# Expert layer of a decoder step: fp32 matmuls replaced by three-product split matmuls, with loads of 256 columns

## The chip, the cores and the metric

The kernel runs on one core of a Trainium2 chip. The metric is the device time of one execution in microseconds (us), taken as the median of several runs. Five engines work beside each other and meet only at semaphores: TensorE (PE, matmuls), VectorE (DVE), ScalarE (ACT), GpSimd (POOL) and SyncE (SP, which here only issues DMA transfers). Each engine takes its own instructions strictly in the order in which they are written.

## The reference

The program is one inference step of a two-layer decoder for 512 prompt tokens and 8 sample tokens (520 in all, 1024 channels). The change touches only the channel mixer of the second layer, a top-2-of-8 mixture of SwiGLU experts:

```python
D_MODEL, N_EXPERTS, TOP_K, D_FF_E = 1024, 8, 2, 1408

def swiglu(h, wg, wu, wd):
    return (jax.nn.silu(h @ wg) * (h @ wu)) @ wd

def moe(h, w_router, wg, wu, wd):
    probs = jax.nn.softmax((h @ w_router).astype(F32), -1)
    top_p, top_i = lax.top_k(probs, TOP_K)
    top_p = top_p / jnp.sum(top_p, -1, keepdims=True)
    gates = jnp.sum(jax.nn.one_hot(top_i, N_EXPERTS, dtype=F32) * top_p[..., None], -2).astype(h.dtype)
    out = jnp.zeros_like(h)
    for e in range(N_EXPERTS):
        out = out + gates[..., e:e + 1] * swiglu(h, wg[e], wu[e], wd[e])
    return out
```

All arrays are float32. An expert has two weight matrices of 1024 x 1408 (gate and up) and one of 1408 x 1024 (down), 16.5 MiB in all.

## The kernel before

Tokens are sorted by expert into slots in DRAM. The experts run in **passes**: a pass takes 176 slots (`SLOTS`) of one expert, and with these inputs there are eight. Every engine has its own loop over the passes (`Fori(0, PASSES)` with `If(p < n_passes)`), written out for all of a pass. Nothing is scheduled: the order on each engine is the order of the code.

A pass works with the tokens transposed (channels on the 128 partitions, 176 columns of tokens):

- 22 **gate and up blocks** (11 pairs, block m = 2f is gate f, m = 2f + 1 is up f). A block is a product of 8 channel slices, each a 128 x 128 weight tile times 128 x 176 tokens (`hTe`), added up in one PSUM bank. ACT applies Silu to the gate bank (L2091) and DVE multiplies it with the up bank (L1739) into `acte`.
- The next pass's rows are transposed into banks 6 and 7 (`expert_tokens`, L1132) and copied to `hTe` by ACT (L2094).
- 8 **down blocks**, each a product of 11 slices with `acte` (L1185). DVE copies each result out of its bank (L1743), PE transposes it (`results`, L1175), ACT copies the rows (L2100), and POOL writes the rows of the pass to DRAM.

The matmuls have float32 operands; one such matmul is two MATMUL instructions, each with a weight load (LDWEIGHTS) of its own. Weights come from SP's queue, one block per transfer, into a ring of 11 slots for gate and up (`w_ring`) and of 4 for down (`d_ring`).

The dense mixer of the first layer, earlier in the program, already has a split form, and the change takes its parts over: ACT copies a weight block rounded to fp32r (`high_part`, L1975), DVE subtracts it from the block (`low_part`, L1467), and PE sums three fp32r products of 260 columns (L841, L843, L845): high weights with high and with low tokens, low weights with high tokens. There POOL splits the activations into high and low (L2191, L2194).

Of the kernel before, what the change touches and what calls it, by code (L numbers as in the profile page):

```python
# [17 lines left out]
F32 = mybir.dt.float32  # L18
# [7 lines left out]
P = 128  # L26
# [45 lines left out]
EXPERT_USES = [6, 5, 6, 5, 4, 4, 6, 6]  # L72
EPS = 1e-6
# [22 lines left out]
def build(nc, a, o):  # L96

    (y_prompt, y_sample, p_delta, p_conv, p_ckv, p_kpe, p_mem_k, p_mem_v, s_delta, s_conv, s_ckv, s_kpe) = o
    with ExitStack() as ctx:
# [22 lines left out]
        xT = sb("xT", [P, KT, T])  # L122
        hT = fixed("hT", [P, KT, T])
        w_ring = fixed("w_ring", [P, WS, KT, P])
        memkT = sb("memkT", [P, 2, 2, MEM])
# [158 lines left out]
        acte, q = place(q, FB, SLOTS)  # L284
        sge, q = place(q, 2, SLOTS)
        yTe, q = place(q, KT, SLOTS)
        yrow, q = place(q, 2, D)
        hTe, q = place(q, KT, SLOTS)
        hrow, q = place(q, 2, D)

# [145 lines left out]
        table_in = sem("table_in")  # L436
        page_rows_ready = sem("page_rows_ready")
# [93 lines left out]
        def last_in(ring, m):  # L531

            first, total = (0, 2 * FB) if m < 2 * FB else (2 * FB, KT)
            i = m - first
            return (m - ring, 0) if i >= ring else (first + max(x for x in range(total) if x % ring == i % ring), 1)

# [3 lines left out]
        def _(pe):  # L540
# [346 lines left out]
            loops["parts"] = 0  # L887
            memory_attention(0)
# [252 lines left out]
            while w_turn[0] % WS:  # L1141
                w_turn[0] += 1
            f0, w0, d0 = loops["experts"] = (list(uses), list(w_uses), [2 * loops["parts"] + 1] * DS)
            per = EXPERT_USES
            pe.wait_ge(routed, 4)
            n_passes = pe.value_load(table[0:1, PASSES:PASSES + 1], min_val=1, max_val=PASSES)
            with pe.Fori(0, PASSES) as p:
                with pe.If(p < n_passes):

                    for k in range(2 * FB):  # L1150
                        s, r = k % WS, k // WS
                        f, bk = k // 2, 2 * (k % 2) + k // 2 % 2
# [13 lines left out]
                    for bk in (2, 3):  # L1166
                        pe.wait_ge(bank_free[bk], p * per[bk] + f0[bk] + per[bk])

                    def results(i):
# [4 lines left out]
                        for r in range(2):  # L1174
                            mm = pe.transpose(bank[bk][0:ROWS, r * P:(r + 1) * P], yTe[:, i, r * ROWS:(r + 1) * ROWS], ident)  # L1175
# [3 lines left out]
                    for i in range(KT):  # L1179
                        s, r = i % DS, i // DS  # L1180
                        bk = 4 + i % 2
                        pe.wait_ge(d_loaded[s], p * 32 + 16 * (d0[s] + r))
                        pe.wait_ge(bank_free[bk], p * 4 + f0[bk] + i // 2)
                        for f in range(FB):
                            mm = pe.matmul(bank[bk][:, 0:SLOTS], d_ring[:, s, f * P:(f + 1) * P], acte[:, f, :],  # L1185
                                           start=(f == 0), stop=(f == FB - 1))
                        mm.then_inc(d_used[s], 1)
# [5 lines left out]
        def _(dve):  # L1193
# [535 lines left out]
            f0, w0, d0 = loops["experts"]  # L1729
            per = EXPERT_USES  # L1730
            with dve.Fori(0, PASSES) as p:
                with dve.If(p < n_passes):

                    dve.wait_ge(d_used[DS - 1], p * 2 + d0[DS - 1])
                    for f in range(FB):
                        k, bg, bu = 2 * f + 1, f % 2, 2 + f % 2
                        dve.wait_ge(w_used[k % WS], p * 2 + w0[k % WS] + k // WS + 1)
                        dve.wait_ge(bank_free[bg], p * per[bg] + f0[bg] + f // 2 + 1)
# [778 lines left out]
```

## Time and profile before

| what | value |
| --- | --- |
| median of 3 runs | 2539.14 us (2539.13 to 2541.26) |
| the profiled execution's own time | 2534.16 us |
| its span, first to last instruction | 2532.5 us |
| PE busy over the span | 2220.1 us (88%) |
| DVE, ACT, POOL busy | 766.9, 468.4, 249.1 us |
| the experts' eight passes | 1814.59 to 2484.60 us of the span |
| mean granted clock of TensorE | 0.902 of full speed |

The profile is one execution. A row that groups instructions gives their count and the mean length of one; lengths overlap where an engine is pipelined, so a rate is read from starts that follow each other. A clock of 1.00 is 2.4 GHz and 0.50 is 1.2 GHz.

### The profile page before, as it was taken

The page shows a single profiled execution, that of the slowest core. Times are in us where ns is not written, and L with a number is a line of the kernel's source. Part 1 is how long each engine was busy: PE and PEld are TensorE (multiplying, and loading weights), DVE is VectorE, ACT ScalarE, POOL GpSimd, SP SyncE. Part 2 cuts the span into 40 slices and gives each one's busy share as a digit, 9 for nine tenths or more (in the row PEclk, how much of TensorE's full clock was granted, in tenths as well). Part 3 has the DMA queues.
Part 4 walks back from the last instruction along what each step waited for, and adds up shares of the span by engine and source line. Part 5 has one row for each costly group of instructions (what it writes and reads, how often), then busy time and mean ns, then how long its engine had stood idle before and what let it go on. Part 6 is the DMA issues. An engine that isn't in the chain of part 4 may idle for free.

```text
span 2532.5 us, 33729 instructions
## 1 busy us (share of the span) xinstructions
PE 2220.1 (88%) x13726; PEld 2007.2 (79%) x13726; DVE 766.9 (30%) x1437; ACT 468.4 (18%) x1020; POOL 249.1 (10%) x332
## 2 busy tenths in 40 slices
PE   5899898976769999997898699997699999999992
PEld 4788787864659999996754577776699999999992
DVE  2245555537232222222224366721100000000003
ACT  1133422203022212211123200101201111111101
POOL 0000101020002302300110033200100000000001
PEclk8899999956789999998898689987799999999996
DMA  7222100030213242342060245520788988898883
GB/s 193 67 67 75 36 1 4 1 95 26 83 34 92 72 113 76 88 113 62 29 231 1 67 166 223 193 75 0 197 217 214 272 208 210 210 273 211 210 204 124
DMA packets 452944, 306.00 MB, mean 121 GB/s; under 512 B 22382, under 2 KB 435457, under 8 KB 448705
## 3 DMA queue, kind: packets, MB, share of 16 engines
q1 hardware_dynamic: 433812, 225.74, 34.0%
q0 software_dynamic: 19024, 78.72, 9.1%
q8 instruction: 81, 1.33, 0.2%
q14 instruction: 27, 0.21, 0.0%
HBM read 276.42 MB, written 28.14 MB: 120 GB/s over the span
## 4 chain that ended last, share of the span: by engine, by line
PE 67%; issue 19%; DVE 6%; POOL 4%; DMA 2%; SPq 1%; ACT 1%; POOLq 0%; DVEq 0%; ACTq 0%
PE bank L1156 17%; PE bank L510 13%; PE bank L1185 8%; PE bank L1062 6%; POOL actL L2194 2%; PE bank L690 2%; PE bank L675 1%; PE bank L685 1%; PE bank L1079 1%; PE bank L548 1%; POOL actH L2191 1%; SPq L2303 1%; PE bank L841 1%; PE bank L845 1%; PE bank L843 1%
## 5 line engine op out<-in xcount | busy, mean ns | idle before, releaser
L1156 PE MATMUL bank<-arena,w_ring 128*128 128x176 f32 x2816 | 424.5, 314 | 4.6 <-issue 4.6
L1156 PEld LDWEIGHTS bank<-arena,w_ring 128*128 128x128 f32 x2816 | 422.4, 191 | 6.6 <-issue 6.6
L510 PE MATMUL bank<-hT,w_ring 128*128 128x260 f32 x1600 | 364.0, 390 | 16.3 <-DVE hT L1208 15.1
L510 PEld LDWEIGHTS bank<-hT,w_ring 128*128 128x128 f32 x1600 | 310.1, 194 | 66.4 <-DVE hT L1208 16.0
L1185 PE MATMUL bank<-arena 128*128 128x176 f32 x1408 | 219.6, 313 | 0.0
L1185 PEld LDWEIGHTS bank<-arena 128*128 128x128 f32 x1408 | 210.2, 190 | 0.0
L1777 ACT ACTIVATE arena<-bank 128x512 f32<-128x512 f32 (+4 forms) x200 | 86.7, 454 | 421.8 <-PE bank L510 226.3
L1739 DVE TENSOR_TENSOR arena<-arena,bank 128x176 f32<-128x176 f32 x88 | 29.7, 337 | 431.4 <-PE bank L1156 431.4
L841 PE MATMUL bank<-hH,gu_high 128*128 128x260 f32 x704 | 142.7, 284 | 18.1 <-DVE w_low L1467 18.1
L1062 PE MATMUL bank<-arena 128*128 128x256 f32 x640 | 151.0, 387 | 3.9 <-DVE arena L1597 3.9
L845 PE MATMUL bank<-hH,w_low 128*128 128x260 f32 x704 | 142.5, 284 | 0.0
L843 PE MATMUL bank<-hL,gu_high 128*128 128x260 f32 x704 | 142.3, 284 | 0.0
L1062 PEld LDWEIGHTS bank<-arena 128*128 128x128 f32 x640 | 118.5, 192 | 26.2 <-issue 9.7
L841 PEld LDWEIGHTS bank<-hH,gu_high 128*128 128x128 f32 x704 | 109.2, 189 | 18.6 <-issue 18.6
L845 PEld LDWEIGHTS bank<-hH,w_low 128*128 128x128 f32 x704 | 109.3, 190 | 0.0
L843 PEld LDWEIGHTS bank<-hL,gu_high 128*128 128x128 f32 x704 | 109.1, 189 | 0.0
L2091 ACT ACTIVATE arena<-bank 128x176 f32<-128x176 f32 x88 | 27.9, 317 | 346.3 <-PE bank L1156 346.2
L1467 DVE TENSOR_TENSOR w_low<-w_ring,gu_high 128x1024 fp32r<-128x1024 f32 x44 | 53.5, 1225 | 113.2 <-ACT gu_high L1975 113.2
L1743 DVE COPY arena<-bank 128x176 f32<-128x176 f32 x64 | 21.9, 342 | 212.3 <-PE bank L1185 212.3
L841 PE MATMUL bank<-actH,d_high 128*128 128x260 f32 x352 | 72.3, 288 | 7.5 <-POOL actL L2194 7.5
L843 PE MATMUL bank<-actL,d_high 128*128 128x260 f32 x352 | 72.2, 287 | 0.0
L845 PE MATMUL bank<-actH,d_low 128*128 128x260 f32 x352 | 72.2, 287 | 0.0
(438 smaller groups left out, 2824.7 us busy)
## 6 DMA issues: line engine op xcount, KB each, us to landing
w_ring<-in_we_gate SPq DMA_DIRECT2D x88, 512.0 KB, 7.2
w_ring<-in_we_up SPq DMA_DIRECT2D x88, 512.0 KB, 7.3
arena<-in_we_down SPq DMA_DIRECT2D x64, 704.0 KB, 6.4
w_ring<-in_w_in_a SPq DMA_DIRECT2D x26, 512.0 KB, 3.7
w_ring<-in_w_gate SPq DMA_DIRECT2D x22, 512.0 KB, 3.8
w_ring<-in_w_up SPq DMA_DIRECT2D x22, 512.0 KB, 3.8
arena<-in_w_down SPq DMA_DIRECT2D x16, 704.0 KB, 6.2
slots<-arena POOLq DMA_DIRECT2D x4, 2560.0 KB, 21.8
```

The source lines that it names most:

```text
L510: mm = pe.matmul(out[i][:, 0:hi - lo], w_ring[:, s, kt, :], rhs[:, kt, lo:hi], start=(kt == 0), stop=(kt == KT - 1))
L690: mm = pe.matmul(b[:, c * P:(c + 1) * P], Xs[:, i, c * P:(c + 1) * P], Einv[:, i, c * P:(c + 1) * P], start=True, stop=True)
L841: pe.matmul(out, w_high, x, start=first, stop=False)
L843: pe.matmul(out, w_high, x, start=False, stop=False)
L845: mm = pe.matmul(out, w_low, x, start=False, stop=last)
L1062: mm = pe.matmul(sc[:, half * GC:(half + 1) * GC], Wq[:, n % 2, blk * P:(blk + 1) * P], block_columns(G, blk), start=(blk == 0), stop=(blk ...
L1156: mm = pe.matmul(bank[bk][:, 0:SLOTS], w_ring[:, s, kt, :], hTe[:, kt, :], start=(kt == 0), stop=(kt == KT - 1))
L1185: mm = pe.matmul(bank[bk][:, 0:SLOTS], d_ring[:, s, f * P:(f + 1) * P], acte[:, f, :], start=(f == 0), stop=(f == FB - 1))
L1467: dve.tensor_tensor(low, raw_block, top.bitcast(F32), ALU.subtract).then_inc(split, 1)
L1739: dve.tensor_tensor(acte[:, f, :], sge[:, f % 2, :], bank[bu][:, 0:SLOTS], ALU.mult)\
L1777: act.activation(dst, b[:, 0:dst.free_size()] if src is None else src(b), func, scale=scale).then_inc(free(key), 1)
L2194: pool.tensor_tensor(actL[:, f, lo:hi], sg[:, f % 2, lo:hi], actH[:, f, lo:hi].bitcast(F32), ALU.subtract)\
```

## The change

The expert products go over to the split form. Tokens and activations are kept as a high and a low half side by side (`eh`, `eact`, 2 x 176 columns). For each slice there are two fp32r matmuls: the high weights with both halves (352 columns, one bank) and the low weights with the high half (176 columns). The two halves of a bank are added when it is read, by a `tensor_reduce` on DVE, which replaces the reads by ACT and the copies by DVE. ACT makes the high weights of every block (five buffers, `ex_high`), DVE the low ones in place of the raw block, both four blocks ahead (`EX_AHEAD`). POOL splits the activations. Loads fetch two blocks at a time (256 columns), six slots for gate and up and three for down. On each engine the semaphore `high_free` counts blocks that PE has finished.

```diff
+EX_SLOTS, EX_DOWN, EX_HIGH, EX_OUT = 6, 3, 5, 4
+EX_AHEAD = 4
@@ PE
+            def expert_product(out, low, top, x, first, last, slot_used):
+
+                if first:
+                    pe.matmul(out[:, 0:2 * SLOTS], top, x.rearrange("p a b -> p (a b)"), start=True, stop=False)
+                mm = pe.matmul(out[:, 0:SLOTS], low, x[:, 0, :], start=False, stop=False)
+                if slot_used is not None:
+                    mm.then_inc(slot_used, 1)
+                if not first:
+                    mm = pe.matmul(out[:, 0:2 * SLOTS], top, x.rearrange("p a b -> p (a b)"), start=False, stop=last)
+                if last:
+                    mm.then_inc(high_free, 1)
-                        pe.wait_ge(w_loaded[s], p * 32 + 16 * (w0[s] + r + 1))
+                        pe.wait_ge(split, p * BLOCKS + split0 + m + 1)
                         pe.wait_ge(bank_free[bk], p * per[bk] + f0[bk] + f // 2)
                         for kt in range(KT):
-                            mm = pe.matmul(bank[bk][:, 0:SLOTS], w_ring[:, s, kt, :], hTe[:, kt, :],
-                                           start=(kt == 0), stop=(kt == KT - 1))
-                        mm.then_inc(w_used[s], 1)
+                            expert_product(bank[bk], low[:, kt, :], top[:, kt, :], eh[:, kt], kt == 0, kt == KT - 1,
+                                           w_used[j % EX_SLOTS] if half and kt == KT - 1 else None)
@@ DVE
+            def block_out(p, i, back=0):
+
+                expert_done(dve, p, 2 * FB + i, back)
+                dve.tensor_reduce(yTe[:, i % EX_OUT, :], halves_of(bank[4 + i % 2]), X, ALU.add).then_inc(bank_free[4 + i % 2], 1)
+
+                    def low_part(m):
+                        raw_block, low, top = expert_parts(m)
+                        dve.wait_ge(high, p * BLOCKS + split0 + m + 1)
+                        dve.tensor_tensor(low, raw_block, top.bitcast(F32), ALU.subtract).then_inc(split, 1)
...
+                    for m in range(BLOCKS):
+                        if m + EX_AHEAD < BLOCKS:
+                            low_part(m + EX_AHEAD)
+                        if m < 2 * FB and m % 2 == 0:
+                            f = m // 2
+                            expert_done(dve, p, m)
+                            dve.tensor_reduce(gate_sum[:, f % 2, :], halves_of(bank[f % 2]), X, ALU.add).then_inc(bank_free[f % 2], 1)
+                        if m < 2 * FB and m % 2:
+                            f = m // 2
+                            bu = 2 + f % 2
+                            expert_done(dve, p, m)
+                            dve.tensor_reduce(up_sum, halves_of(bank[bu]), X, ALU.add).then_inc(bank_free[bu], 1)
+                            dve.wait_ge(bank_free[bu], p * per[bu] + f0[bu] + f // 2 + 1)
+                            dve.wait_ge(gate_silu, p * FB + f + 1)
+                            dve.tensor_tensor(sge[:, f % 2, :], sge[:, f % 2, :], up_sum, ALU.mult).then_inc(gated, 1)
...
+                        if m > 2 * FB:
+                            block_out(p, m - 2 * FB - 1)
@@ ACT
+                    def high_part(m):
+                        raw_block, _, top = expert_parts(m)
+                        expert_loaded(act, p, m)
+                        act.wait_ge(high_free, p * BLOCKS + m + 1)
+                        act.activation(top, raw_block, ACT.Copy).then_inc(high, 1)
...
+                    for m in range(BLOCKS):
+                        if m + EX_AHEAD < BLOCKS:
+                            high_part(m + EX_AHEAD)
+                        if m < 2 * FB and m % 2 == 0:
+                            f = m // 2
+                            act.wait_ge(bank_free[f % 2], p * per[f % 2] + f0[f % 2] + f // 2 + 1)
+                            act.wait_ge(act_split, p * FB + loops["act0"] + f - 1)
+                            act.activation(sge[:, f % 2, :], gate_sum[:, f % 2, :], ACT.Silu).then_inc(gate_silu, 1)
...
+                        if m >= 2 * FB + 2:
+                            rows_of_block(p, m - 2 * FB - 2)
@@ POOL
+                        pool.tensor_tensor(eactH[:, f, :], sge[:, f % 2, :], ones[:, 0:1].to_broadcast([P, SLOTS]), ALU.mult)\
+                            .then_inc(pool_step, 1)
...
+                        pool.tensor_tensor(eactL[:, f, :], sge[:, f % 2, :], eactH[:, f, :].bitcast(F32), ALU.subtract)\
+                            .then_inc(act_split, 1)
@@ SP
+                    for j in range(KT // 2):
+                        s, r = j % EX_DOWN, j // EX_DOWN
+                        sp.wait_ge(d_used[s], p * EX_DUSES[s] + d0[s] + r)
+                        load(down_slots[s][0], columns("we_down", j * 2 * P, (j + 1) * 2 * P), d_loaded[s])
```

The order of instructions on three engines shows what now stands between what. First ACT in the gate and up blocks of a pass, before (each row an instruction; L2091 is the Silu of a gate bank, REGISTER_ALU sets the value of a wait):

```order
L2090 ISA [waits w_used0]
L2091 ACT_TABLE_LOAD
L2091 ACTIVATE arena<-bank 128x176 [waits bank_free2]
L2090 ISA [waits w_used2]
L2091 ACTIVATE arena<-bank 128x176 [waits bank_free3]
```

and of the change at the same place (L2220 is `high_part`, from the fifth block of the pass on; L2234 is Silu):

```order
L2220 ACTIVATE ex_high_81<-gu_pair_63 128x1024 [waits high_free]
L2232 ISA
L2233 ISA [waits bank_free0]
L2234 ACT_TABLE_LOAD
L2234 ACTIVATE arena<-gate_sum 128x176 [waits act_split]
L2219 REGISTER_ALU [waits w_loaded3]
L2220 ACTIVATE ex_high_77<-gu_pair_65 128x1024 [waits high_free]
L2219 REGISTER_ALU [waits w_loaded2]
L2220 ACTIVATE ex_high_78<-gu_pair_63 128x1024 [waits high_free]
L2232 ISA
L2233 REGISTER_ALU [waits bank_free1]
L2234 ACTIVATE arena<-gate_sum 128x176 [waits act_split]
```

Two high parts now stand between one Silu and the next. Then DVE in the same stretch, before (L1739 is the product of Silu and up bank):

```order
L1738 ISA [waits w_used1]
L1739 TENSOR_TENSOR arena<-arena,bank 128x176 [waits bank_free0]
L1738 ISA [waits w_used3]
L1739 TENSOR_TENSOR arena<-arena,bank 128x176 [waits bank_free1]
L1738 REGISTER_ALU [waits w_used5]
```

and of the change (L1834 is `low_part`, L1848 the sum of a gate bank's halves, L1853 of an up bank's, L1856 their product):

```order
L1834 TENSOR_TENSOR gu_pair_low<-gu_pair_63,ex_high_81 128x8x128 [waits high]
L598 REGISTER_ALU
L1848 TENSOR_REDUCE gate_sum<-bank 128x176 [waits high_free]
L1833 REGISTER_ALU
L1834 TENSOR_TENSOR gu_pair_low<-gu_pair_65,ex_high_77 128x8x128 [waits high]
L598 REGISTER_ALU
L1853 TENSOR_REDUCE up_sum<-bank 128x176 [waits high_free]
L1854 ISA
L1855 ISA [waits bank_free2]
L1856 TENSOR_TENSOR arena<-arena,up_sum 128x176 [waits gate_silu]
L1833 REGISTER_ALU
L1834 TENSOR_TENSOR gu_pair_low<-gu_pair_63,ex_high_78 128x8x128 [waits high]
```

Where one product stood for each two blocks, two low parts, two sums and a product stand now. Last SP at the end of a pass of the change, the four loads of down weights:

```order
L2454 DMA down_pair_71<-in_we_down 128x11x256 [waits d_used0]
L2608 REGISTER_ALU
L2454 DMA down_pair_73<-in_we_down 128x11x256 [waits d_used1]
L2454 DMA down_pair_75<-in_we_down 128x11x256 [waits d_used2]
L2608 REGISTER_ALU
L2454 DMA down_pair_71<-in_we_down 128x11x256 [waits d_used0]
```

The fourth goes into the slot of the first (`down_pair_71`), and the next pass's gate loads stand behind it.

## Rows read from the trace of the kernel before

**Rows 1.** The page: the span, and PE's busy time.
```profile
span 2532.5 us, 33729 instructions
PE 2220.1 (88%) x13726; PEld 2007.2 (79%) x13726; DVE 766.9 (30%) x1437; ACT 468.4 (18%) x1020; POOL 249.1 (10%) x332
```
**Rows 2.** The chain of waits, second pass: start us, length us, engine, line, instructions.
```profile
1900.36 52.77 PE bank L1156 x352
1954.86 6.60 PE bank L1185 x44
```
**Rows 3.** Busy time by windows, that pass: PE, PEld, DVE, ACT, POOL, clock, DMA.
```profile
1900.36:1983.69 83.33, 82.50 (x560) 81.62 (x561) 6.45 (x19) 9.40 (x25) 1.45 (x2) 1.00 0.88 225
```
**Rows 4.** Timeline of the dense split products, 260 columns, two instructions a row.
```profile
900.07 0.40 PE L843 MATMUL bank<-actL,d_high 128*128 128x260 f32 x2
900.31 0.40 PE L845 MATMUL bank<-actH,d_low 128*128 128x260 f32 x2
```
**Rows 5.** Instructions by line: duration ns min/median/max, first and last start us.
```profile
L845 PEld LDWEIGHTS bank<-hH,w_low x704: 187/188/331, 754.9 to 1080.9; 128*128 128x128 f32 x176
...
L636 PEld LDWEIGHTS bank<-rstd,sel x24: 181/187/187, 159.2 to 161.8; 12*128 12x128 f32 x24
L636 PE MATMUL bank<-rstd,sel x24: 251/251/272, 159.2 to 161.8; 12*128 12x8 f32 x24
```
**Rows 6.** DVE by line and shape, the dense mixer's low parts and the product.
```profile
L1467 DVE TENSOR_TENSOR w_low<-w_ring,gu_high x44: 1216/1225/1226, 752.6 to 1065.8; 128x1024 fp32r<-128x1024 f32 x44
L1467 DVE TENSOR_TENSOR d_low<-arena,d_high x16: 1624/1626/1925, 872.2 to 1136.0; 128x1408 fp32r<-128x1408 f32 x16
...
L1739 DVE TENSOR_TENSOR arena<-arena,bank x88: 336/337/340, 1822.1 to 2453.3; 128x176 f32<-128x176 f32 x88
```
**Rows 7.** DVE sums out of PSUM by shape: busy us, mean ns, idle before.
```profile
L1550 DVE TENSOR_REDUCE small<-bank 128x1 f32<-128x384 f32 x6 | 3.3, 557 | 0.2
L1550 DVE TENSOR_REDUCE small<-bank 128x1 f32<-128x256 f32 x6 | 2.5, 424 | 0.2
```
**Rows 8.** ACT by line: dense high parts, Silu, table load.
```profile
L1975 ACT ACTIVATE gu_high<-w_ring x44: 1040/1064/1064, 749.8 to 1064.7; 128x1024 fp32r<-128x1024 f32 x44
L1975 ACT ACTIVATE d_high<-arena x16: 1379/1382/1382, 867.2 to 1134.6; 128x1408 fp32r<-128x1408 f32 x16
...
L2091 ACT ACTIVATE arena<-bank x88: 317/317/318, 1821.0 to 2450.9; 128x176 f32<-128x176 f32 x88
L2091 ACT ACT_TABLE_LOAD  x8: 1283/1283/1283, 1819.7 to 2403.1; - x8
```
**Rows 9.** Timeline of the dense mixer: a high part, two products, the low part.
```profile
1023.75 1.06 ACT L1975 ACTIVATE gu_high<-w_ring 128x1024 fp32r<-128x1024 f32 x1 [4.13 <-PE bank L845]
1023.78 0.76 DVE L1480 TENSOR_TENSOR arena<-arena,bank 128x260 f32<-128x260 f32 x2 [2.90 <-PE bank L845]
...
1024.85 1.23 DVE L1467 TENSOR_TENSOR w_low<-w_ring,gu_high 128x1024 fp32r<-128x1024 f32 x1 [0.31 <-ACT gu_high L1975]
```
**Rows 10.** SP's queue, 1814 to 2485 us (512 B packets): packets, MB, share of 16 engines.
```profile
q1 hardware_dynamic: 270828, 136.74, 80.6%
```
**Rows 11.** SP's queue, 1400 to 1445 us (1 KB packets), the same columns.
```profile
q1 hardware_dynamic: 3264, 3.15, 22.8%
```
**Rows 12.** The page's DMA issues: KB each, median us from issue to landing.
```profile
w_ring<-in_w_in_a SPq DMA_DIRECT2D x26, 512.0 KB, 3.7
```
**Rows 13.** Timeline of PE after a wait in the dense mixer.
```profile
886.70 0.48 PE L841 MATMUL bank<-actH,d_high 128*128 128x260 f32 x2 [3.77 <-POOL actL L2194]
```
**Rows 14.** Windows behind that wait, and in and behind another; columns as in rows 3.
```profile
887.70:891.00 3.30, 3.30 (x17) 3.30 (x16) 0.00 (x0) 0.00 (x0) 0.00 (x0) 0.50 0.00 0
1167.50:1175.00 7.50, 0.00 (x0) 0.00 (x0) 7.46 (x9) 0.00 (x0) 0.00 (x0) 0.50 0.00 0
1175.00:1181.00 6.00, 5.93 (x14) 4.68 (x15) 0.01 (x1) 0.00 (x0) 0.00 (x0) 0.50 0.00 0
```
**Rows 15.** POOL's low half of 260 activations in the dense mixer.
```profile
L2194 POOL TENSOR_TENSOR actL<-arena,actH 128x260 fp32r<-128x260 f32 x44 | 52.3, 1189 | 3.4
```

More of the change, by code:

```diff
@@ L72 @@
 EXPERT_USES = [6, 5, 6, 5, 4, 4, 6, 6]
+EX_SLOTS, EX_DOWN, EX_HIGH, EX_OUT = 6, 3, 5, 4
+EX_PAIRS = FB // 2
+EX_LOADS = 2 * EX_PAIRS + 1
+EX_AHEAD = 4
+EX_USES = [len(range(s, EX_LOADS, EX_SLOTS)) for s in range(EX_SLOTS)]
+EX_DUSES = [len(range(s, KT // 2, EX_DOWN)) for s in range(EX_DOWN)]
 EPS = 1e-6
@@ L1728, in _ @@
             n_passes = dve.value_load(table[0:1, PASSES:PASSES + 1], min_val=1, max_val=PASSES)
-            f0, w0, d0 = loops["experts"]
+            f0, _, _ = loops["experts"]
+            split0 = loops["parts"] * BLOCKS
             per = EXPERT_USES
+            for g in range(4):
+                dve.wait_ge(h_high, KT + g + 1)
+                b = filled(dve, ("hx", g))
+                dve.tensor_tensor(ehL[:, 2 * g:2 * g + 2, :], b[:, 0:2 * SLOTS].rearrange("p (a b) -> p a b", a=2),
+                                  ehH[:, 2 * g:2 * g + 2, :].bitcast(F32), ALU.subtract)\
+                   .then_inc(free(("hx", g)), 1)
@@ L1732, in _ @@
                 with dve.If(p < n_passes):
[L1734 to L1738, printed above, removed]
-                        dve.tensor_tensor(acte[:, f, :], sge[:, f % 2, :], bank[bu][:, 0:SLOTS], ALU.mult)\
-                           .then_inc(bank_free[bu], 1)
@@ new lines, in _ @@
+                    for m in range(EX_AHEAD):
+                        high_part(m)
+                    with act.If(p > 0):
+                        for i in range(KT - 2, KT):
+                            rows_of_block(p, i, back=1)
+                    for m in range(BLOCKS):
[6 more added lines that the diff above has]
+                            act.activation(sge[:, f % 2, :], gate_sum[:, f % 2, :], ACT.Silu).then_inc(gate_silu, 1)
+                        if m == 2 * FB - 1:
+                            for g in range(4):
+                                act.wait_ge(hx, p * 4 + 4 + g + 1)
+                                act.activation(ehH[:, 2 * g:2 * g + 2, :], bank[6 + g % 2][:, 0:2 * SLOTS].rearrange("p (a b) -> p a b", a=2),
+                                               ACT.Copy).then_inc(h_high, 1)
+                            act.wait_ge(rows_out, p * 16 + 16 * ZFILL)
+                        if m >= 2 * FB + 2:
+                            rows_of_block(p, m - 2 * FB - 2)
@@ L2103, in _ @@
+            for i in range(KT - 2, KT):
+                rows_of_block(n_passes, i, back=1)
             for t in range(NT + 1):
@@ L2430, in _ @@
             load(gfin, a["g_final"].partition_broadcast(P), gfin_in)
-            f0, w0, d0 = loops["experts"]
+            w0, d0, _ = loops["ex_loads"]
             sp.wait_ge(spread, 160)
+            for s in range(WS):
+                sp.wait_ge(w_used[s], w0[s])
             sp.wait_ge(routed, 4)
```

159 lines of the change are left out of this document (110 added, 49 removed).

## Prediction

> **What bounds the kernel now.** I read the page first: of a span of 2532.5 us PE is busy for 88% [rows 1]. Then the chain of waits in order of time, which shows where the end is set. From 1814.59 to 2484.60 us (the table above) it is almost PE alone, eight passes alike: 352 gate and up MATMULs in 52.77 us, then the down blocks [rows 2]. The windows of the second pass show the rest: a pass lasts 83.33 us, PE works in 82.50 of them at full clock, DVE in 6.45, ACT in 9.40, POOL in 1.45 [rows 3]. So today a pass is PE's work and the other engines have over 70 us to spare. What the change gives back on PE, and what it asks of DVE and ACT, decides.
>
> **PE's work.** One old MATMUL takes 52.77 / 352 = 0.150 us. A float32 product of one slice is two of them, 0.299 us (without the last one's tail). A pass has 22 x 8 + 8 x 11 = 264 such products, 79.0 us; transposes and waits make up the other 4.3.
>
> The new product is an fp32r MATMUL of 352 columns and one of 176. Neither is in the trace. The nearest fp32r rows are the dense ones: starts 0.24 us apart for two of 260 columns, 0.120 each [rows 4]. Wide: scaled by columns 0.162; the old instruction, which takes 0.150 and streams 176 columns twice, gives the lower end. I take 0.155. Narrow: scaled by columns 0.081, the lower end. But each MATMUL has a weight load of its own, and a float32 matmul of only 8 columns still follows the last after (161.8 - 159.2) / 23 = 0.113 us. The fp32r load lasts as long as that one's, 188 against 187 ns [rows 5]. I take 0.113, since narrow matmuls are nearest; the upper end is the float32 rate, 0.299. One product is then 0.268 us (0.231 to 0.454), a pass 264 x 0.268 = 70.8 us on PE, 8.2 less than now.
>
> The Trainium skill, "TensorE: Matmul & The Clock Gate", section LDWEIGHTS, puts a load at its columns divided by 1.2 per ns: an estimate of 0.107 us for 128 columns, whatever the matmul streams. By it alone the product would be 0.262 us, by column counts alone 0.243, and the pass of the first rival below 1.6 us or 6.6 us shorter. The float32 rows agree with it (0.113); no row shows a narrow fp32r matmul.
>
> **DVE's and ACT's work.** Durations: a low part 1.225 us, 1.626 for a down block, the product at most 0.337 [rows 6]. A sum of halves reads 352 elements out of PSUM; 256 take 0.424 and 384 take 0.557, so 0.52 on that line (0.34 if it cost only what 176 cost, 0.8 if its strided pairs cost half as much again) [rows 7]. A high part takes 1.064 or 1.382, Silu 0.317, a table load 1.283 [rows 8]. An instruction that waits on another engine starts 0.03 us behind its end (1023.75 + 1.06 to 1024.85), and one that waits for nothing starts 0.08 before the last one's end (two products of 0.42 in 0.76) [rows 9].
>
> Added up, DVE has 22 x 1.14 + 8 x 1.54 + 30 x 0.44 + 11 x 0.26 + 4 x 0.44 (the low tokens) = 55 us a pass, ACT 41 without its twelve copies. Either would fit beside PE. But they wait for each other. In front.md's order, DVE can't sum up-bank m + 1 before low part m + 5; that needs high part m + 5, which stands on ACT behind Silu of gate m, which needs DVE's sum of gate m. So from one gate sum's end to the next:
>
> Silu 0.03 + 0.24; high part 1.06; low part 0.03 + 1.15; up sum 0.52; product 0.03 + 0.26; second low part 1.15; gate sum 0.52: together 4.99 us for two blocks. PE needs 16 x 0.268 = 4.29. The loop is longer, so the gate and up blocks run at DVE's and ACT's pace, with PE waiting for low parts (PE's spare 0.7 us a loop hides the narrow matmul's price too).
>
> **A pass, in order:**
> - From the last down block to the first gate sum: table 1.28, high 1.06, low 1.25, block 0 with 8 x 0.268 = 2.14, sum 0.52: 6.3 us.
> - Ten loops 50.0; half a loop with a long high and low part to the last product, 4.0; three more low parts and one more high part of down size, 1.5: 55.5. PE runs four blocks ahead, so it finishes its last up block about two loops before DVE gets there, and stands still for some 10 us: the next tokens' low halves stand behind all that on DVE, and PE's transposes wait for their banks.
> - Two low halves and PE's last transposes: 1.6.
> - Down: 88 x 0.268 = 23.6, seven results at 0.22 = 1.5, and 1.5 of waits, since the sum of a down block stands behind the low part of one five blocks later: 26.6.
> - The fourth down load (1408 KB) goes into the first one's slot, so SP issues it only when PE has done the second down block. With 512 B packets SP's queue needs 0.806 x 671 x 16 / 270828 = 0.032 us a packet [rows 10]; with 1 KB, the new size, 0.228 x 45 x 16 / 3264 = 0.050, 326 GB/s [rows 11]. So the load takes 4.4 us and the 1.65 by which an unhurried 512 KB load exceeds its 2.05 of transfer [rows 12]. Then come its high part 1.38, low part 1.55, and only behind that the sum which frees a bank for PE: 9.7 us in all, of which PE covers 4.0 with its third down block. Wait: 5.7.
> - Clock: after 3.77 us of idling PE ran at 1.2 GHz for the next 3.3 us, after a longer idle for 6 [rows 13, 14]. Each pass now has one idle of some 10 and one of 5.7 us, followed by blocks on the path: half of 6 + 3.3 is 4.7, and I take 4.0, because a part falls on blocks that wait anyway.
>
> Sum: 6.3 + 55.5 + 1.6 + 26.6 + 5.7 + 4.0 = 99.7 us against 83.33, 16.4 more, times eight 131; the first pass starts 2.4 later (high and low part in front of PE). Span 2532.5 + 133 = 2666. The execution's own time is 2534.16, and the median of the three runs is 4.98 above that, so I forecast 2539.14 + 133 = 2672 us.
>
> **Costed at nothing.** The other transfers: 16.5 MiB at 326 GB/s are 53 us of a pass of 100; if 1 KB rows went no faster than 512 B ones, 68, still hidden. POOL's two operations for each pair: at 260 columns the longer takes 1.19 us on average beside DVE [rows 15], so under 2.4 of a loop of 5.0; Silu waits only for those of two pairs before. POOL's wait for the rows written out falls on the start of the next pass, where Silu first needs it two loops later.
>
> **Rivals.**
> - *PE sets the pace after all (faster).* If a loop takes less than PE's 4.29 us, the pass is 70.8 + 4.3 + 1.0 for the low tokens = 76.1, and without the late load 8 x -7.2 + 2.4 = -55: 2484 us. For it: DVE's own part of a loop is only 3.6 us, and PE is the engine that waits for nobody now [rows 3]. Against it: the missing 1.4 is Silu and a high part, both durations from rows, and in-order queues leave no way round. Chance 0.09. With the late load and its clock but no loop the pass is 76.1 + 5.7 + 1.7 = 83.5, no change: 0.04.
> - *The loop, but no late load.* If the fourth load lands in time, 5.7 and 1.7 of clock go: pass 92.3, 8 x 9.0 + 2.4 = +74, 2613 us. For it speaks only that the transfer could start earlier than I read. 0.17.
> - *Sums of strided pairs at 0.8 us.* Two more terms of 0.28 in each loop: +6.5 a pass, 2724 us. 0.09.
> - *Narrow fp32r at the float32 rate.* 264 x 0.454 + 5.3 = 125.2 us a pass, PE bound: 8 x 41.9 = +335, 2874 us. No row speaks for it except that all fp32r here has 260 columns. 0.06.
> - My forecast: 0.55; by the ends of its terms (clock 0 to 4.7, narrow 0.081 to 0.120, handoffs to 0.1) 2635 to 2700.
>
> **How the numbers follow.** From the second rival's 2613 less 23 for its own terms, to the third's 2724 plus 16, the range 2590 to 2740 holds 0.55 + 0.17 + 0.09 = 0.81. Below it lie the cases where PE sets the pace, above it the narrow matmuls. About 0.2% is what a measurement of this kernel tells from no change: faster 0.09, same 0.04, slower 0.87.
>
> **What the profile after would show.** Right: passes of some 100 us; low parts on DVE released by ACT's high parts, and Silu by DVE's sums; gate sums 5.0 us apart; PE idle before the last transposes by about 10 us and before the fourth down block by about 6; the clock at 0.50 behind both. Wrong: PE busy through the gate blocks, starts of gate sums 4.3 us apart or less, or narrow matmuls that follow each other at 0.3 us. The forecast falls with the loop: if Silu or the high parts turn out to run ahead of DVE, the sign turns.

## The result and the profile after

The changed kernel takes 2711.99 us (median of four runs, 2710.94 to 2713.12), the kernel before 2539.14 us on the same chip: a ratio of 1.068, 95% interval 1.0665 to 1.0702. It is slower by 172.85 us, inside the predicted range (2590 to 2740) and 40 us above the predicted time.

The page of the changed kernel; its two lines answer to [rows 1]:

```profile
span 2710.7 us, 35689 instructions
PE 2231.0 (82%) x13726; PEld 2007.2 (74%) x13726; DVE 1179.1 (43%) x1889; ACT 731.2 (27%) x1268; POOL 420.9 (16%) x508
```

PE has as many instructions as before, and DVE 412 us and ACT 263 us more to do. Windows of the second pass, columns as in [rows 3], which they answer to; then 34 us of its gate and up blocks, and its stretches of idle PE with what follows each:

```profile
1929.00:2034.57 105.57, 84.87 (x562) 82.86 (x562) 57.71 (x76) 42.23 (x55) 22.96 (x25) 0.87 0.58 178
1938.00:1972.00 34.00, 34.00 (x247) 33.88 (x247) 23.15 (x33) 15.61 (x21) 13.15 (x14) 1.00 1.01 300
1981.20:1991.50 10.30, 0.02 (x1) 0.02 (x1) 7.28 (x10) 4.58 (x6) 2.78 (x3) 0.67 0.00 0
1992.00:1998.00 6.00, 6.00 (x29) 6.00 (x27) 2.67 (x3) 2.20 (x3) 0.19 (x1) 0.50 0.00 0
2005.60:2011.50 5.90, 0.02 (x1) 0.02 (x1) 2.13 (x3) 2.91 (x3) 0.00 (x0) 0.75 1.10 350
2012.00:2015.00 3.00, 3.00 (x14) 3.00 (x14) 1.40 (x2) 0.38 (x1) 0.00 (x0) 0.50 1.10 347
2029.50:2033.10 3.60, 0.79 (x4) 0.19 (x2) 3.60 (x4) 3.16 (x5) 0.00 (x0) 0.91 0.00 0
2033.20:2037.00 3.80, 3.80 (x16) 3.80 (x16) 2.48 (x3) 1.12 (x2) 0.77 (x1) 0.50 0.28 66
```

A pass lasts 105.57 us against 83.33. PE is idle for 10.3 us ahead of the last transposes and for 5.9 ahead of the fourth down block, with the clock at 0.50 behind both, as forecast. Between the passes there is a third stop: PE works for 0.79 us of the 3.6 from 2029.50 on, all of it transposes. The forecast had that stop as well, but not that the next pass's first block runs at half clock behind it (the last row).

One sign that the forecast had named for being wrong does show: PE is busy through most of the gate and up blocks (34.00 us of 34.00 in the second row). It isn't what sets the pace there. The gate sums are 5.14 us apart all the same, while PE needs 4.4 us for two blocks (measured below). At the start of a pass the low parts are some four blocks ahead of PE, and PE works that lead off; only in the last two or three loops of a pass (six in the first pass) does it stop, for 0.5 us each. Experiments 2 and 4 test this.

The timeline shows why PE stops (start us, length us, engine, line). First the fourth down load, then the end of one pass and the start of the next, then one loop of the gate and up blocks (from 2268.23 on):

```profile
2001.31 0.37 SPq L2454 DMA_DIRECT2D down_pair<-in_we_down  x1
2007.96 1.38 ACT L2220 ACTIVATE ex_high<-down_pair 128x1408 fp32r<-128x1408 f32 x1 [8.05 <-DMA down_pair<-in_we_down]
2009.37 1.62 DVE L1834 TENSOR_TENSOR down_pair_low<-down_pair,ex_high 128x1408 fp32r<-128x1408 f32 x1 [7.37 <-ACT ex_high L2220]
2010.91 0.52 DVE L1827 TENSOR_REDUCE yTe<-bank 128x176 f32<-128x352 f32 x1
2011.48 0.66 PE L1251 MATMUL bank<-CF,yTe 128*88 128x128 f32 x2 [5.92 <-DVE yTe L1827]
...
2027.10 1.28 ACT L2220 ACT_TABLE_LOAD   x1 [0.20 <-issue]
2029.48 2.36 DVE L1834 TENSOR_TENSOR gu_pair_low<-gu_pair,ex_high 128x1024 fp32r<-128x1024 f32 x2 [2.67 <-ACT ex_high L2220]
2031.76 0.52 DVE L1827 TENSOR_REDUCE yTe<-bank 128x176 f32<-128x352 f32 x1
2032.33 0.62 PE L1251 MATMUL bank<-CF,yTe 128*88 128x128 f32 x2 [2.66 <-DVE yTe L1827]
...
2038.19 1.28 ACT L2234 ACT_TABLE_LOAD   x1 [3.87 <-DVE gate_sum L1848]
...
2268.23 1.22 DVE L1834 TENSOR_TENSOR gu_pair_low<-gu_pair,ex_high 128x1024 fp32r<-128x1024 f32 x1
2268.40 1.39 POOL L2424 TENSOR_TENSOR eact<-arena,CF 128x176 fp32r<-128x176 f32 x1 [3.10 <-DVE arena L1856]
2269.37 0.52 DVE L1848 TENSOR_REDUCE gate_sum<-bank 128x176 f32<-128x352 f32 x1
2270.00 0.35 ACT L2234 ACTIVATE arena<-gate_sum 128x176 f32<-128x176 f32 x1 [2.89 <-DVE gate_sum L1848]
2270.25 1.04 ACT L2220 ACTIVATE ex_high<-gu_pair 128x1024 fp32r<-128x1024 f32 x1
2271.33 1.23 DVE L1834 TENSOR_TENSOR gu_pair_low<-gu_pair,ex_high 128x1024 fp32r<-128x1024 f32 x1 [1.44 <-ACT ex_high L2220]
2272.47 0.52 DVE L1853 TENSOR_REDUCE up_sum<-bank 128x176 f32<-128x352 f32 x1
2273.11 0.34 DVE L1856 TENSOR_TENSOR arena<-arena,up_sum 128x176 f32<-128x176 f32 x1
2273.37 1.22 DVE L1834 TENSOR_TENSOR gu_pair_low<-gu_pair,ex_high 128x1024 fp32r<-128x1024 f32 x1
2274.50 0.52 DVE L1848 TENSOR_REDUCE gate_sum<-bank 128x176 f32<-128x352 f32 x1
```

Read the loop from the gate sum of 2269.37 downwards: Silu waits for the sum, the high part stands behind Silu on ACT's queue, the low part waits for the high part ("1.44 <-ACT ex_high"), the up sum stands behind the low part, and the next gate sum comes 5.13 us after the first. That is the forecast's loop, 4.99 there. Two handoffs are longer than taken: Silu starts 0.11 us behind the gate sum's end and the product 0.12 behind the up sum's, where 0.03 was assumed.

### The profile page after: what moved, and what is told of

Read it like the earlier page. It is cut to its first block, busy times and chain, and to the rows that moved or that the text cites. A ratio compares the mean times of both kernels' runs of the same rounds, so it can differ in the third digit from the quotient of the medians.

```text
span 2710.7 us, 35689 instructions
## 1 busy us (share of the span) xinstructions
PE 2231.0 (82%) x13726; PEld 2007.2 (74%) x13726; DVE 1179.1 (43%) x1889; ACT 731.2 (27%) x1268; POOL 420.9 (16%) x508
## 4 chain that ended last, share of the span: by engine, by line
PE 49%; issue 23%; DVE 12%; ACT 5%; DMA 5%; POOL 3%; SPq 1%; DVEq 1%; ACTq 0%; POOLq 0%
PE bank L537 12%; PE bank L1221 6%; PE bank L1126 5%; ACT ex_high L2220 4%; PE bank L1217 3%; DVE gu_pair_low L1834 2%; DMA down_pair<-in_we_down 2%; POOL actL L2336 2%; DVE up_sum L1853 1%; PE bank L753 1%; PE bank L738 1%; PE bank L748 1%; PE bank L1143 1%; DVE gate_sum L1848 1%; PE bank L611 1%
## 5 line engine op out<-in xcount | busy, mean ns | idle before, releaser
L1221 PE MATMUL bank<-eh,ex_high 128*128 128x352 f32 x1232 | 367.9, 366 | 0.0
L1217 PE MATMUL bank<-eh,gu_pair_low 128*128 128x176 f32 x1408 | 327.9, 254 | 0.0
L1217 PEld LDWEIGHTS bank<-eh,gu_pair_low 128*128 128x128 f32 x1408 | 274.3, 198 | 0.0
L1834 DVE TENSOR_TENSOR gu_pair_low<-gu_pair,ex_high 128x1024 fp32r<-128x1024 f32 x176 | 212.9, 1221 | 137.5 <-ACT ex_high L2220 137.5
L1221 PEld LDWEIGHTS bank<-eh,ex_high 128*128 128x128 f32 x1232 | 240.8, 195 | 0.0
L1221 PE MATMUL bank<-eact,ex_high 128*128 128x352 f32 x640 | 204.0, 388 | 0.0
L1217 PE MATMUL bank<-eact,down_pair_low 128*128 128x176 f32 x704 | 176.9, 267 | 0.0
L2220 ACT ACTIVATE ex_high<-gu_pair 128x1024 fp32r<-128x1024 f32 x176 | 175.3, 1044 | 2.1 <-DMA gu_pair<-in_we_up 2.0
L1834 DVE TENSOR_TENSOR down_pair_low<-down_pair,ex_high 128x1408 fp32r<-128x1408 f32 x64 | 103.8, 1622 | 116.8 <-ACT ex_high L2220 116.8
L1217 PEld LDWEIGHTS bank<-eact,down_pair_low 128*128 128x128 f32 x704 | 152.0, 219 | 0.0
L1126 PEld LDWEIGHTS bank<-arena 128*128 128x128 f32 x640 | 119.4, 193 | 26.6 <-issue 9.7
L2220 ACT ACTIVATE ex_high<-down_pair 128x1408 fp32r<-128x1408 f32 x64 | 86.8, 1369 | 90.1 <-DMA down_pair<-in_we_down 65.0
```

Source lines behind the costliest of these rows:

```text
L1126: mm = pe.matmul(sc[:, half * GC:(half + 1) * GC], Wq[:, n % 2, blk * P:(blk + 1) * P], block_columns(G, blk), start=(blk == 0), stop=(blk ...
L1217: mm = pe.matmul(out[:, 0:SLOTS], low, x[:, 0, :], start=False, stop=False)
L1221: mm = pe.matmul(out[:, 0:2 * SLOTS], top, x.rearrange("p a b -> p (a b)"), start=False, stop=last)
L1834: dve.tensor_tensor(low, raw_block, top.bitcast(F32), ALU.subtract).then_inc(split, 1)
L2220: act.activation(top, raw_block, ACT.Copy).then_inc(high, 1)
```

## Experiments

Each run was timed beside the kernel before (medians 2534 to 2535 us on those chips, against 2539.14 beside the changed kernel), so medians that differ by a few us from the changed kernel's don't decide, and the traces do. Line numbers in a fence are those of its own kernel.

**1. A fourth down slot** (four_down_slots). Five pair slots for gate and up, four for down, so that the fourth down load waits for nobody.

```
-EX_SLOTS, EX_DOWN, EX_HIGH, EX_OUT = 6, 3, 5, 4
+EX_SLOTS, EX_DOWN, EX_HIGH, EX_OUT = 5, 4, 5, 4
...
+        down_at = [("arena", q + i * FB * 2 * P * 4) for i in range(EX_DOWN - 1)] + [("w_ring", EX_SLOTS * pair)]
```

> The changed kernel with a fourth slot for down weights (and five instead of six for gate and up), so that the fourth down load no longer waits for the second down block. Theory A (an in-order loop of DVE and ACT sets the pace of the gate and up blocks, and the late fourth load stops PE in the down blocks): the 6.1 us for which PE stands before the fourth down block go, and with them some 2 us of half clock behind them, 8 us in each of eight passes, 2712 - 64 = 2648 us; the gate sums stay 5.14 us apart. Theory B (PE sets the pace: fp32r products dearer than they look): no change, 2712. Theory C (the transfers as such are too slow): no change, the wait moves to another load.

Measured: 2667.34 us, ratio 1.0528 (1.0511 to 1.0546), 45 us less than the changed kernel. The 5.9 us stop is gone from every pass, so the late load is shown; the stop ahead of the transposes stays at 10.3. The gain is smaller than expected. ACT's high parts now wait for pair loads (9.9 us in the four passes from the third, none in the changed kernel's), the price of having one pair slot less.

**2. Silu behind the next block's high part** (silu_after_high). On ACT, Silu of a gate block moves from the gate block's place to the up block's, one high part later; DVE waits for the product before it overwrites the up sum.

```
                             expert_done(dve, p, m)
+                            if f:
+                                dve.wait_ge(gated, p * FB + f)
                             dve.tensor_reduce(up_sum, halves_of(bank[bu]), X, ALU.add).then_inc(bank_free[bu], 1)
...
-                        if m < 2 * FB and m % 2 == 0:
+                        if m < 2 * FB and m % 2:
                             f = m // 2
...
                             act.activation(sge[:, f % 2, :], gate_sum[:, f % 2, :], ACT.Silu).then_inc(gate_silu, 1)
```

> The changed kernel with one thing moved on ACT: Silu of a gate block stands behind the next block's high part instead of ahead of it (and DVE waits, long satisfied, for its own product before it overwrites the up sum). Theory A: the loop is cut, DVE's own part of it is 3.6 us, so PE sets the pace of the gate blocks: gate sums 16 x 0.272 = 4.35 us apart instead of 5.14, ten loops 8 us, and the 10 us for which PE stands before the last transposes shrink, with the half clock behind them another 4 us: 12 us a pass, about 2612 us. The wait for the fourth down load stays at 6 us. Theory B and theory C: no change, 2712.

Measured: 2607.56 us, ratio 1.0284 (1.0267 to 1.0301), 104 us less. The timeline of ACT and DVE in a loop:

```profile
2216.41 1.06 ACT L2222 ACTIVATE ex_high<-gu_pair 128x1024 fp32r<-128x1024 f32 x1 [1.14 <-PE bank L1221]
2216.44 0.52 DVE L1848 TENSOR_REDUCE gate_sum<-bank 128x176 f32<-128x352 f32 x1
2217.38 0.33 ACT L2236 ACTIVATE arena<-gate_sum 128x176 f32<-128x176 f32 x1
2220.86 0.52 DVE L1848 TENSOR_REDUCE gate_sum<-bank 128x176 f32<-128x352 f32 x1
```

Gate sums are 4.42 us apart, and the high part is released by PE ("1.14 <-PE bank"): PE sets the pace (16 products of 0.275 us are 4.40), and the idle ahead of the transposes shrinks from 10.3 to 1.7 us. So the loop was the order of two instructions on one queue, not the amount of work on DVE or ACT.

**3. Both** (silu_after_high_four_slots).

> Both edits together. Theory A: the two gains add up, 20 us a pass, 2712 - 160 = 2552 us, within 1% of the kernel before the change; a pass of 84 us, of which PE is busy some 76. Theory B: 2712. Theory C: 2712, with waits for loads.

Measured: 2560.55 us, ratio 1.0101 (1.0084 to 1.0117). It is 151 us below the changed kernel, the two alone gave 45 and 104: they add up (by the ratios 148, 40 and 101), so the loop and the late load are separate causes. Windows of the fifth pass, then three stretches in it:

```profile
2168.10:2256.90 88.80, 82.77 (x562) 81.45 (x562) 58.21 (x77) 43.34 (x55) 30.62 (x25) 0.92 0.70 211
2219.00:2220.92 1.92, 0.01 (x1) 0.00 (x0) 1.80 (x5) 0.56 (x2) 1.36 (x2) 1.00 0.55 133
2221.00:2227.60 6.60, 6.60 (x30) 6.60 (x31) 2.98 (x4) 2.20 (x3) 0.55 (x1) 0.50 1.10 359
2255.20:2261.60 6.40, 6.13 (x24) 6.13 (x25) 3.91 (x5) 2.90 (x4) 0.77 (x1) 0.50 0.39 105
```

In this pass a stop of 1.92 us is followed by 6.6 us of work at half clock, and one of 2.62 us between the passes by 6.4 us, nearly all of it work. Passes two to six are alike in this.

**4. Few narrow products** (few_narrow_products, one run). It leaves out the low weights' product in every slice of a block but the last.

```
-                mm = pe.matmul(out[:, 0:SLOTS], low, x[:, 0, :], start=False, stop=False)
+                if last:
+                    mm = pe.matmul(out[:, 0:SLOTS], low, x[:, 0, :], start=False, stop=False)
```

> The changed kernel without the narrow matmuls (low weights with high tokens) of all slices but the last of each block: 30 of 264 a pass are left, so the low weights' product is left out of the result for the other slices. Theory A: in the gate blocks nothing is gained, gate sums stay 5.14 us apart, since PE waits there anyway; in the down blocks 80 x 0.11 = 9 us a pass go, of which the late load takes back 1: about 2650 us. Theory B: 234 x 0.11 = 26 us a pass, about 2506 us.

Measured: 2637.62 us. PE has 1872 instructions fewer; the loop doesn't change. PE's timeline in it:

```profile
2231.41 0.43 PE L1216 MATMUL bank<-eh,ex_high 128*128 128x352 f32 x1 [0.31 <-DVE gate_sum L1849]
2231.68 1.13 PE L1222 MATMUL bank<-eh,ex_high 128*128 128x352 f32 x6
2232.65 0.24 PE L1218 MATMUL bank<-eh,gu_pair_low 128*128 128x176 f32 x1
2234.61 0.63 PE L1216 MATMUL bank<-eh,ex_high 128*128 128x352 f32 x1 [1.52 <-DVE up_sum L1854]
```

Gate sums are still 5.14 us apart; PE now has stops of 1.5 us through the gate and up blocks, where the changed kernel has its few of 0.5. With the narrow matmuls nearly all gone the kernel is still 4% slower than before, so PE's work was not what made it slower. In the second pass the stretch from the first gate sum to the transposes takes 59.0 us in both kernels. The 74 us come from the rest, the down blocks and the next pass's first block (36.5 us instead of 46.6), where PE's own work counts.

The run also prices the narrow matmul. Wide ones alone follow each other at (2232.65 - 2231.68) / 6 = 0.162 us. In the changed kernel, with a narrow one between:

```profile
2267.84 0.35 PE L1221 MATMUL bank<-eh,ex_high 128*128 128x352 f32 x1
2268.03 0.24 PE L1217 MATMUL bank<-eh,gu_pair_low 128*128 128x176 f32 x1
2268.11 0.36 PE L1221 MATMUL bank<-eh,ex_high 128*128 128x352 f32 x1
2268.31 0.24 PE L1217 MATMUL bank<-eh,gu_pair_low 128*128 128x176 f32 x1
2268.39 0.35 PE L1221 MATMUL bank<-eh,ex_high 128*128 128x352 f32 x1
```

From wide to wide 0.275 us: the narrow one costs 0.113, where columns alone would make it 0.081. Starts alone would mislead: 0.08 behind a narrow one and 0.19 behind a wide one. What the narrow one costs beyond its columns shows in front of it, as 0.03 more behind the wide one.

**5. A spread pass** (spread_pass): experiment 3, and a new order around the down blocks, to take the 1.9 and 2.6 us stops away.

```
-                        if i:
-                            results(i - 1)
+                        if i == 0:
+                            pe.wait_ge(hrow_in, p * 16 + 32)
+                        if i < 2:
+                            next_tokens(2 * i)
+                            next_tokens(2 * i + 1)
+                        else:
+                            results(i - 2)
...
                         if m > 2 * FB:
                             block_out(p, m - 2 * FB - 1)
+                            if m + EX_AHEAD < BLOCKS:
+                                low_part(m + EX_AHEAD)
```

(ACT's rows of a block and the low halves of the next tokens move to match.)

> Silu behind the next block's high part and four down slots, as in the third run, and the order of the down stage changed as well: the next tokens' transposes stand behind the first two down blocks instead of ahead of them, results two blocks behind their block, DVE sums a down block before it makes the next low part, ACT copies most rows in the next pass. Theory A (each PE gap of 1.9 to 2.6 us in that run also costs half of the 6.8 us of half clock behind it): gaps and half clock go together, a pass falls from 90.8 us by 4.9 and by up to 10.2, span falls by 80 to 120: 2440 to 2480 us. Theory B (only the gaps themselves count; the half clock falls where PE waits anyway, or comes as well without gaps): 8 x 4.9 = 39 less, about 2521 us.

Measured: 2509.30 us, ratio 0.990 (0.9883 to 0.9917): faster than the kernel before. The fifth pass:

```profile
2135.60:2214.50 78.90, 76.21 (x560) 75.39 (x560) 57.93 (x76) 42.89 (x56) 30.34 (x24) 1.00 0.80 238
```

Against experiment 3's 88.80 us the pass is 9.9 shorter. PE stops for 2.7 us instead of 6.0 in all (3.3 less). It works for 76.2 us instead of 82.8 (6.6 less), since two stretches of half clock, with some 13 us of work in them, are gone. So the half clock was on the path, as theory A has it and B doesn't. But the kernel falls short of A's range: I had counted a third stretch of half clock in a pass that has two, and taken the pass as 90.8 us. Nor do stops and half clock simply go together: every pass still stops for 1.6 to 2.3 us in the first down block, and five of the eight have no half clock behind it. The run moves several things at once, and which of them did how much isn't separated.

**6. The same with three down slots** (spread_pass_three_slots): six pair slots and three down slots, as in the changed kernel.

> The order of the down stage and Silu's place as in the run before, but the changed kernel's own six pair slots and three down slots, so that the fourth down load is still issued only behind the second down block. Theory A (the load was waited for because the sum that frees a bank stood behind its low part; with the sum ahead of it PE has four blocks, 12 us, to cover 9.7): the 5.7 us wait is gone without the fourth slot, within 10 us of the run before. Theory B (the load is late for PE itself): a wait of some 5 us and its half clock in each pass, 45 to 70 us above the run before.

Measured: 2542.35 us, ratio 1.0022 (1.0009 to 1.0035), 33 us above experiment 5: neither theory. The timeline at the fourth load:

```profile
2217.78 0.37 SPq L2466 DMA_DIRECT2D down_pair<-in_we_down  x1
2224.39 1.38 ACT L2229 ACTIVATE ex_high<-down_pair 128x1408 fp32r<-128x1408 f32 x1 [5.29 <-DMA down_pair<-in_we_down]
2225.81 1.62 DVE L1839 TENSOR_TENSOR down_pair_low<-down_pair,ex_high 128x1408 fp32r<-128x1408 f32 x1 [5.64 <-ACT ex_high L2229]
2227.35 0.52 DVE L1832 TENSOR_REDUCE yTe<-bank 128x176 f32<-128x352 f32 x1
2227.92 0.43 PE L1216 MATMUL bank<-eact,ex_high 128*128 128x352 f32 x1 [2.92 <-DVE yTe L1832]
```

The sum that frees a bank still stands behind the late low part on DVE, only that of the next block. The new order buys one block's product, 11 x 0.275 = 3.0 us, and the stop goes from 5.9 to 2.9. My expectation had four blocks.

**7. Narrow loads** (narrow_loads): each pair of blocks as two transfers of 512 B rows.

```
-                            load(dst, columns("we_up" if j % 2 else "we_gate", lo, lo + 2 * P), w_loaded[s])
+                            for x in range(2):
+                                load(dst[:, :, x * P:(x + 1) * P], columns("we_up" if j % 2 else "we_gate", lo + x * P, lo + (x + 1) * P), w_loaded[s])
```

> The changed kernel with each pair of weight blocks loaded as two transfers of 512 B rows instead of one of 1 KB rows; nothing else changed. Theory A (loads are hidden in the gate and up blocks and only the fourth down load is on the path): that load of 2816 rows of 512 B takes longer, 16 x 176 x 2 x 0.032 / 16 = 5.6 us against 4.4, so 1.2 to 2 us a pass: 2722 to 2728 us. Rival B (the wider rows carry the transfers of the whole pass): 68 us of transfers become the bound nowhere, but if rows of 512 B are slower beside the high and low parts than read, gate loads are late too: 2740 us or more. Rival C (two transfers run beside each other and gain what the rows lose): 2712 us, no change.

Measured: 2721.37 us, ratio 1.0735 (1.0717 to 1.0753), so the wider loads are worth about 9 us. The profiled runs' spans differ by 8.4 us, and their traces show where. First the fourth down load, as theory A has it: from the issue of its first transfer to its high part it takes 7.25 us on average against 6.72, and PE's stop lengthens from 6.0 to 6.5 us on average. Passes two to seven take 3.9 us more together, 0.65 each, less than A's 1.2 to 2. Secondly the first pass, whose loads nothing hides. Here the fifth high part waits for its load; in the changed kernel (second line) the sixth does:

```profile
1829.45 1.06 ACT L2218 ACTIVATE ex_high<-gu_pair 128x1024 fp32r<-128x1024 f32 x1 [5.91 <-DMA gu_pair<-in_we_gate]
...
1828.49 2.01 ACT L2220 ACTIVATE ex_high<-gu_pair 128x1024 fp32r<-128x1024 f32 x2 [2.02 <-DMA gu_pair<-in_we_up]
```

The first gate sum comes at 1831.7 instead of 1824.2, but the next interval is shorter, 6.4 us instead of 8.6, so that at the second pass's first gate sum 4.9 us are left. The first weight load was issued 2.2 us later to begin with (1807.43 against 1805.18), which an earlier stage brought; some 2.7 us are the first pass's.

**8. One table load a pass** (one_table_load): a Silu of one column ahead of a pass's first high part.

```
+                    act.wait_ge(high_free, p * BLOCKS + 1)
+                    act.activation(silu_of_one, ones[:, 0:1], ACT.Silu)
                     for m in range(EX_AHEAD):
                         high_part(m)
```

> The changed kernel with a Silu of one column at the start of each pass, so that Silu's table is loaded there and the second table load of a pass, ahead of the first Silu, goes. Theory A (that second load, 1.28 us, is on the loop, since the first gate sum interval is 6.44 us and the others 5.14): 8 x 1.3 = 10 us less, 2702 us, first interval 5.14. Rival (it only moves: the start of the pass is longer by as much as the first interval is shorter): 2712 us, no change.

Measured: 2707.06 us, ratio 1.0668 (1.0647 to 1.0689); the interval overlaps the changed kernel's, so the time doesn't decide. In the passes the load is gone. Where the changed kernel has a table load at 2038.19 behind the gate sum, this one has Silu itself:

```profile
2040.10 0.35 ACT L2237 ACTIVATE arena<-gate_sum 128x176 f32<-128x176 f32 x1 [3.86 <-DVE gate_sum L1849]
```

Its first gate sum interval is 5.16 us, and passes two to seven take 104.0 on average against 105.0: about 1 us each, 8 together.

**9 and 10. The last pair first** (last_pair_first), **and with one table load** (last_pair_first_one_table). On top of experiment 5, the last activations go ahead of a down block's high and low part.

```
+                            if m == 2 * FB - 1:
+                                low_part(m + EX_AHEAD)
```

> The order of the fifth run (Silu late, four down slots, spread down stage), and the last gate/up pair goes ahead of the low and high part of the down block that stood before it on DVE and ACT, since there PE still waits 1.6 to 2.3 us inside the first down block for the last activations. Theory A (that gap is on the path): the up sum no longer stands behind a 1.62 us low part, the gap shrinks to 0.5 us or less, 8 x 1.2 to 1.6 = 10 to 13 less than the fifth run: 2496 to 2500 us. Rival (GpSimd's split, 1.8 us beside DVE's low part against 0.48 alone, takes up what is gained, or the delayed down block is late instead): 2505 to 2512 us, no change.

> The order of the run before, and the Silu of one column at the start of each pass that takes the second table load away. In this order PE waits 0.4 us or less at the start of a pass, and Silu stands a pair behind, so theory A says that the table load is hidden: within 4 us of the run before. Rival (it is on the path as in the changed kernel): 8 to 10 us less.

Measured: 2504.95 us, ratio 0.9876 (0.9857 to 0.9896), and 2505.09 us, ratio 0.989 (0.9874 to 0.9907). Both intervals overlap that of experiment 5, so neither step is shown to gain. In experiment 9 the stop in the first down block is 0.9 to 1.0 us or less in four passes and 2.3 in the other four. What takes the gain up is seen on POOL and DVE, here in a pass with a stop of 0.9 us:

```profile
2193.78 0.48 POOL L2443 TENSOR_TENSOR eact<-arena,CF 128x176 fp32r<-128x176 f32 x1 [0.84 <-DVE arena L1866]
2194.17 3.52 DVE L1842 TENSOR_TENSOR down_pair_low<-down_pair,ex_high 128x1408 fp32r<-128x1408 f32 x2 [0.47 <-ACT ex_high L2234]
2194.34 1.87 POOL L2446 TENSOR_TENSOR eact<-arena,eact 128x176 fp32r<-128x176 f32 x1
```

POOL's second operation, which PE waits for, started beside a low part and took 1.87 us; it takes 0.55 where DVE is idle. In the fourth pass, with its stop of 2.3 us, both POOL operations start beside a low part and take 1.95 and 1.82 us.

## Why the prediction was right, and where it was off

From the end of the first gate sum of the second pass (1932.52) to that of the third (2038.10), the predicted pass against the measured one:

| piece of a pass | predicted us | measured us |
| --- | --- | --- |
| ten loops, to the last product | 55.5 | 58.5 |
| low tokens and transposes | 1.6 | 1.9 |
| down blocks, late load, clock | 26.6 + 5.7 + 4.0 = 36.3 | 36.5 |
| last down block to the first gate sum | 6.3 | 8.7 |
| pass | 99.7 | 105.6 |

Passes start 105.4 us apart on average. The difference of 5.7, times eight, is 46 us; with it the forecast's span of 2666 becomes 2712, and the span is 2710.7. Part of that agreement is luck: at the start of a pass and in the down blocks terms match or cancel for reasons that the forecast didn't have (below).

- **The loop** was right as a mechanism, by experiment 2 (taken away: 104 us) and experiment 4 (PE relieved, loop unchanged). Its size was off by 0.15 us for the two handoffs behind a sum, some 1.6 us a pass.
- **A second table load** is the term that was missing. I took the row of one load a pass [rows 8] as the load of the new kernel too. But there the first operation of a pass is now a Copy and Silu comes later, and each is preceded by a load of 1.283 us. The Trainium skill, "ScalarE activation tables: per-element evaluation and per-set limits", section "Table sets in the compiler and the runtime", says that the compiler's back end places the loads block by block; the trace agrees, with 8 loads at either line. Experiment 8 removed the second with one instruction. In the table this is 1.3 us of the first piece.
- **The start of a pass** took 2.4 us more: 3.7 us without products, and then block 0 at half clock, 4.98 us to the end of the sum instead of 2.7. The forecast's own sum had PE stand for 3.6 us there, but its clock term counted only the other two stops; that is the term that was too small. That 3.7 is so near 3.6 is luck. The table load begins at 2027.10, 2.3 us before the last down block ends. What PE waits for is the sum of that block, which stands on DVE behind two low parts of the next pass, and whose transposes stand on PE ahead of block 0.
- **The down blocks** came out at 36.5 us for 36.3 because their terms cancel. The products take 24.2 us instead of 23.6, the late load 5.9 instead of 5.7 and the half clock 4.6 (9.2 us of work) instead of 4.0, but the other waits are 0.7 instead of 1.5, and some 1.1 is left for the results instead of 1.5.
- **The late load** was right: 6.65 us from issue to the high part (2001.31 to 2007.96) against the estimated 6.05, a stop of 5.9 us against 5.7; experiment 1 removed it by an additional slot. The 0.050 us a packet was a little low: 192 of the 3264 packets of [rows 11] have under 512 B, and the trace's packets of 1 KB take 0.053 us, before and after.
- **PE's product** was taken as 0.155 + 0.113 = 0.268 us; it takes 0.162 + 0.113 = 0.275. Scaling the wide part by columns, the upper end, was right, and so was the narrow matmul's floor [rows 5]. The loop hides it all in the gate blocks. The estimate of 0.107 from the Trainium skill, "TensorE: Matmul & The Clock Gate", section LDWEIGHTS, is 5% below the 0.113 measured.
- **The sum of halves** was taken as 0.52; it is 0.517 (L1848 and L1853 in the windows' pass), so its rival at 0.8 is out, as is the float32 rate.
- **PE sets the pace after all**, the rival on the other side, prices PE's work rightly and describes this kernel wrongly. With the loop and the load undone (experiment 5) PE works for 76.2 us a pass, and that rival had 76.1 for the whole pass, which takes 78.9. The kernel is then 1% faster than before. The change is no loss in itself; its order and its three down slots are.
- **"POOL costed at nothing"** holds in the changed kernel (1.38 + 0.56 us in a loop of 5.14) and no longer in experiments 5 and 9, where PE sets the pace and the first down block waits for POOL.
- **A slip without effect**: ACT's rows [rows 8] add up to 39 us a pass, not 41. Either fits beside PE, and the loop doesn't use it.

## What to carry to other kernels

Where a change gives work to engines that have time to spare, adding up busy time isn't enough: follow one block round through every in-order queue, and see whether the ring of waits is shorter than the bound engine's time for the same blocks. An engine that is busy all the time need not set the pace: here PE was, for most of the gate and up blocks, while the loop of DVE and ACT did. One instruction, placed one position too early on ACT's queue, cost 104 us, and a transfer slot too few 45. Where the bound engine stops, even for 2 us, look for half clock behind the stop as well; here it came behind some of these stops and not behind others.

## What the runs showed of the hardware

- In experiment 3, stops of 1.92 and 2.62 us were followed by 6.6 and 6.4 us at half clock. In experiment 5, five of the eight stops in a first down block (1.63 to 2.00 us) had none behind them, and the other three (1.63, 1.87 and 2.26 us) had 3.4 us. So the length of the stop alone doesn't decide, and what does isn't settled here.
- A POOL operation of 176 columns takes 0.48 us, and 1.39 us when it starts 0.17 us into a low part on DVE: it ends 0.34 us behind that low part's end (2269.79, 2269.45), as if most of its work had only then begun. The Trainium skill, "SBUF — State Buffer", section "Who interferes with whom", says that a DVE instruction with two SBUF inputs, which a low part is, contends with a GpSimd instruction that reads SBUF; the trace agrees.
